# Router on the un-normalised sum, LayerNorm's scale and shift at evictions, a fourth likely expert

## What is computed

```python
h = layer_norm(ALPHA * h + mix, ln_g[i, 0], ln_b[i, 0])
ffn = hier_moe(h, group_w, group_b, expert_w, expert_b, gate_w, up_w, down_w)
h = layer_norm(ALPHA * h + ffn, ln_g[i, 1], ln_b[i, 1])

def hier_moe(t, ...):                      # 4 groups of 8 experts, D_FF = 512
    g_logits = t @ group_w + group_b       # the best group of each token
    g_prob = softmax(g_logits)             # its probability: g_val
    e_logits = t @ expert_w + expert_b     # within the group: the best two of 8
    top_p = softmax(top_v) * g_val
    hid = silu(t @ gate_w[e]) * (t @ up_w[e])
    out = sum over the token's two experts of top_p * (hid @ down_w[e])
```

## Time and profile before

| | |
|---|---|
| time, three runs | 1208.69, 1208.34, 1207.22 us |
| the profiled execution's own time | 1208.71 us |
| its span, first to last instruction | 1206.9 us |
| mean granted TensorE clock | 0.981 |
| TensorE busy | 1123.4 us (93%) |
| VectorE busy | 456.8 us (38%) |
| ScalarE busy | 318.2 us (26%) |
| GpSimd busy | 224.0 us (19%) |
| DMA moved | 427.14 MB |

### The profile page before, as it was taken

One profiled execution on the slowest core, in us unless ns is written; L12 is line 12 of the kernel. 1 busy time (PEld: TensorE's weight loads), 2 busy tenths in 40 slices (PEclk: granted clock), 3 DMA queues, 4 the chain that ended last, 5 costly groups with the idle time before them and its releaser, 6 DMA issues.

```text
span 1206.9 us, 16477 instructions
## 1 busy us (share of the span) xinstructions
PE 1123.4 (93%) x5664; PEld 665.5 (55%) x5664; DVE 456.8 (38%) x933; ACT 318.2 (26%) x590; POOL 224.0 (19%) x117
## 2 busy tenths in 40 slices
PE   8999999999999898899989899999999998899995
PEld 6998778643334444444343488875444454445552
DVE  3775773633322222222222344556332222222224
ACT  5578962221111011111111165632211111111110
POOL 2366775300000000000000388333000000000000
PEclk9999999999999999999999999998999999999998
DMA  9723559799999999999999933397999999999994
GB/s 367 288 105 113 201 193 367 277 370 398 432 428 427 430 428 428 428 429 428 428 428 424 413 116 140 140 370 320 390 410 430 428 428 428 429 428 428 428 425 188
DMA packets 35114, 427.14 MB, mean 354 GB/s; under 512 B 3728, under 2 KB 5936, under 8 KB 8064
## 3 DMA queue, kind: packets, MB, share of 16 engines
q1 hardware_dynamic: 32640, 416.13, 83.1%
q10 hardware_dynamic: 2240, 9.66, 2.2%
q0 software_dynamic: 192, 0.79, 0.4%
HBM read 424.69 MB, written 1.87 MB: 353 GB/s over the span
## 4 chain that ended last, share of the span: by engine, by line
PE 64%; DMA 22%; DVE 9%; ACT 2%; issue 2%; POOL 1%; ACTq 0%; SPq 0%; DVEq 0%; POOLq 0%
PE bank L844 26%; DMA ring<-in_gate_w 19%; PE bank L906 11%; PE bank L1009 4%; PE bank L592 3%; PE bank L728 3%; PE bank L1098 2%; DMA ring<-in_kv_w 2%; DMA reach_down<-in_down_w 1%; PE bank L1007 1%; PE bank L680 1%; PE bank L891 1%; PE bank L821 1%; DVE arena L1701 1%; PE bank L709 1%
## 5 line engine op out<-in xcount | busy, mean ns | idle before, releaser
L844 PE MATMUL bank<-ring,arena 128*64 128x512 f32 x928 | 417.2, 603 | 16.0 <-DMA ring<-in_gate_w 16.0
L906 PE MATMUL bank<-reach_down,arena 128*64 (+1 forms) x464 | 211.0, 607 | 29.1 <-DVE arena L1898 28.1
L541 POOL TENSOR_TENSOR split_ring<-ring,split_ring 128x1024 fp32r<-128x1024 f32 x56 | 138.5, 2503 | 461.9 <-ACT split_ring L534 456.7
L844 PE MATMUL bank<-reach_gate,arena 128*64 (+1 forms) x464 | 214.2, 610 | 0.0
L906 PE MATMUL bank<-ring,arena 128*64 128x512 f32 x464 | 210.7, 607 | 0.0
L844 PE MATMUL bank<-reach_up,arena 128*64 (+1 forms) x464 | 205.5, 595 | 0.0
L844 PEld LDWEIGHTS bank<-ring,arena 128*64 128x64 f32 x928 | 124.7, 138 | 134.9 <-issue 103.3
L1922 DVE TENSOR_TENSOR arena<-arena,bank 128x512 f32<-128x512 f32 x116 | 72.3, 682 | 194.8 <-PE bank L892 194.8
L906 PEld LDWEIGHTS bank<-reach_down,arena 128*64 128x64 f32 x464 | 61.9, 139 | 112.4 <-issue 102.5
L1915 DVE SCALAR_TENSOR_TENSOR split_arena<-bank,arena,split_arena 128x512 fp32r<-128x512 f32 x58 | 43.4, 750 | 150.0 <-ACT split_arena L1453 150.0
L844 PEld LDWEIGHTS bank<-reach_up,arena 128*64 128x64 f32 x464 | 60.9, 136 | 61.4 <-issue 60.5
(11 more groups left out here) (301 smaller groups left out, 1375.7 us busy)
## 6 DMA issues: line engine op xcount, KB each, us to landing
reach_gate<-in_gate_w SPq DMA_DIRECT2D x29, 2048.0 KB, 17.5
reach_up<-in_up_w SPq DMA_DIRECT2D x29, 2048.0 KB, 20.3
reach_down<-in_down_w SPq DMA_DIRECT2D x29, 2048.0 KB, 21.1
ring<-in_down_w SPq DMA_DIRECT2D x27, 2048.0 KB, 16.9
ring<-in_gate_w SPq DMA_DIRECT2D x25, 2048.0 KB, 17.9
ring<-in_up_w SPq DMA_DIRECT2D x25, 2048.0 KB, 16.8
ring<-in_in_w SPq DMA_DIRECT2D x9, 2048.0 KB, 21.5
ring<-in_out_w SPq DMA_DIRECT2D x4, 2048.0 KB, 9.1
```

Source lines behind the costliest of these rows:

```text
L541: unit.tensor_tensor(split_ring[:, j % RING, here], ring[:, j % RING, here], split_ring[:, (j + 1) % RING, here], ALU.subtract).then_inc(d ...
L844: last = mm(bank[out_bank][64 * e:64 * e + 64, :], exT[:, k, 64 * e:64 * e + 64], w, start=k == 0, stop=k == KD - 1)
L906: last = mm(bank[5 + c][64 * e:64 * e + 64, :], hidT[:, k, 64 * e:64 * e + 64], w, start=k == 0, stop=k == 3)
```

## The change

- The router multiplies the un-normalised sum ALPHA * h + mix. TensorE transposes it as soon as each quarter is added (`turn_mixed`, counted by `h_mixed`), all four copies out of PSUM are ScalarE's. `best_group` puts mean and deviation back with two instructions: the logits are (x @ w - mean * column sums of w) * rstd + folded bias. The column sums are a new reduction in `scale_router` and a new product in `fold_sum`.
- Gathered and sorted tokens are the normalised ones without scale and shift; these are applied where the tokens leave PSUM (`copy_exT`, now four instructions each on ScalarE and VectorE instead of one, and `store_sorted`). The old scalings at L1177, L1179, L1806 and L1812 go.
- ALPHA * (x * g + b) is made by VectorE in `residual` (two instructions for each 128 tokens); ScalarE's L1478 goes. The tokens' rest (L1194 on GpSimd) becomes `rest_of_tokens` on VectorE. Both are put in between other work of VectorE.
- The rows of scale and shift go to another home, and in layer 0 their load is issued after the last square of the SSD instead of with x.
- A fourth likely expert: `likely_fourth`, three rounds of five small instructions, for both layers. SyncE loads pair 1's second expert (the fourth likely one) and pair 2's first in interleaved halves (`first_halves`), and waits for the list by a signal given before `route`.
- `keep_clock` has five products instead of three before `rank`, and the ones between the last output blocks and the router go. GpSimd's preparation for the sort waits for `sel`.

```diff
...
@@ -412,6 +419,18 @@
     sp.dma_start(home, w[L, bass.ds(expert, 1), :, here].rearrange("e p x -> p (e x)")).then_inc(done, 16)
+
+def first_halves(L, base, before, kind, second, next_first):
+
+    j, ahead_j = slab_at(base, kind, 1), slab_at(base, kind, 0)
+    other = two_homes(sp, kind, 2)
+    for half in range(2):
+        here = slice(half * SLOT // 2, (half + 1) * SLOT // 2)
+        sp.wait_ge(w_used, before * 12 + (12 + 2 * (base - RING) + 4 * kind + 2 * half + 2))
+        fetch(L, second, kind, ring[:, j % RING, here], w_second[j % RING] if half else w_full[j % RING], here)
+        if half:
+            sp.wait_ge(w_full[ahead_j % RING], before * 16 + (32 + 16 * (ahead_j // RING)))
+        fetch(L, next_first(), kind, other[:, here], w_full[ahead_j % RING] if half else w_ahead, here)
@@ -442,7 +461,7 @@
 sp.wait_ge(moe[L]["first"], L + 1)
-return guesses(sp, L, 3)
+return guesses(sp, L, 4)
@@ -457,18 +476,27 @@
 sp.wait_ge(moe[L]["logit"], TB * (L + 1))
-sp.wait_ge(h_ready, 2 * L + 1)
 ahead(L, base, before, 1, 2, guess[2])
-sp.wait_ge(moe[L]["route"], L + 1)
-further = further_pairs(sp, L)
 def expert(i):
-def rest_of_pair(q, second, next_first=None, edge=None):
+def second_pair():
+    listed = []
+
+    def fifth():
+        if not listed:
+            sp.wait_ge(moe[L]["listed"], 2 * L + 2)
+            listed.append(expert(slice(4, 5)))
+        return listed[0]
+
+    for kind in range(2):
+        first_halves(L, base, before, kind, guess[3], fifth)
+    slab_of_pair(L, base, before, 1, 2, 1, guess[3])
+    ahead(L, base, before, 2, 2, fifth())
+
+def rest_of_pair(q, second, next_first=None):
     for kind in range(3):
-        slab_of_pair(L, base, before, q, kind, 1, second,
-                     halves=edge == ("last" if kind == 2 else "first"))
+        slab_of_pair(L, base, before, q, kind, 1, second)
         if next_first is not None:
@@ -478,8 +506,10 @@
+second_pair()
+sp.wait_ge(moe[L]["route"], L + 1)
+further = further_pairs(sp, L)
 turning = further * 2 // 3
-rest_of_pair(1, expert(slice(3, 4)), expert(slice(4, 5)), "first")
 with sp.Fori(1, turning - 1) as p:
@@ -645,7 +675,8 @@
 pe.wait_ge(fold_row, L + 1)
-mm(bank[3][:, 0:RC], ones, folded[:, L * RC:(L + 1) * RC], start=True, stop=True).then_inc(fold_mm, 1)
+mm(bank[3][:, 0:RC], ones, folded[:, L * RC:(L + 1) * RC], start=True, stop=True)
+mm(bank[3][:, 64:64 + RC], ones, less_sums[L], start=True, stop=True).then_inc(fold_mm, 1)
@@ -748,29 +779,34 @@
     for half in range(2):
-        if t == 0:
-            pe.wait_ge(hT_a, 7 * L + half + 1)
-        else:
-            pe.wait_ge(hT_v if half else hT_a, 3 * L + 1 if half else 7 * L + 3)
+        pe.wait_ge(hT_a, 8 * L + 2 * t + half + 1)
         for k in range(4 * half, 4 * half + 4):
-def turn_normed(L, t):
-
-    pe.wait_ge(xn_ready, 2 * L * TB + t + 1)
-    for k in range(KD):
-        b = bank[t_bank(2 * L) + 2 * t + k // 4]
+def turn_mixed(L, t, half):
+
+    pe.wait_ge(h_mixed, 2 * TB * L + 2 * t + half + 1)
+    for k in range(4 * half, 4 * half + 4):
+        b = bank[t_bank(2 * L) + 2 * t + half]
         last = nc.tensor.transpose(b[:, (k % 4) * P:(k % 4 + 1) * P], h[:, t, k * P:(k + 1) * P], ident)
-        if k % 4 == 3:
-            last.then_inc(hT_mm, 1)
+        if L == 0 and t == 0 and k == 0:
+            last.then_inc(w_used, 4)
+    last.then_inc(hT_mm, 1)
+
+def turn_and_route(L):
+
+    for t in range(TB):
+        for half in range(2):
+            turn_mixed(L, t, half)
+    for t in range(TB):
+        router_logits(L, t)
 last_blocks(1, 0)
-turn_normed(0, 0)
 def keep_clock(n, b):
@@ -781,9 +817,6 @@
 last_blocks(1, 1)
-keep_clock(1, 3).then_inc(w_used, 4)
-router_logits(0, 0)
-keep_clock(1, 3)
...
@@ -921,7 +957,7 @@
 m = moe[L]
-keep_clock(3, 6)
+keep_clock(5, 6)
 pe.wait_ge(m["mask"], L + 1)
@@ -935,7 +971,7 @@
 keep_clock(1, 6)
-pe.wait_ge(h_ready, L * 2 + 1)
+pe.wait_ge(xn_ready, 4 * L + TB)
 gather(L, 0)
...
@@ -1172,26 +1204,21 @@
-pool.wait_ge(ln_in, 32 * (n + 1))
+pool.wait_ge(ln_in, 32)
 pool.wait_ge(hT_mm, turned)
 last = T(h[:, t, :], h[:, t, :], lnw[:, 1, :], ALU.add)
-if n != 1:
-    last.then_inc(h_first, 1)
-elif t == TB - 1:
+if t == TB - 1:
     last.then_inc(h_ready, 1)
 m = moe[L]
-pool.wait_ge(mix_mm, 2 * TB * (L + 1))
+pool.wait_ge(m["sel"], L + 1)
 pool.memset(arena[:, lower_at + TB * D:lower_at + TB * D + CAP], 0.0)
   cst[:, C_BLK:C_BLK + 8].unsqueeze(2).to_broadcast([P, 8, CAP]), ALU.add).then_inc(m["low"], 1)
-pool.wait_ge(m["high"], L + 1)
-pool.wait_ge(m["route"], L + 1)
-T(h_low, h, h_high, ALU.subtract).then_inc(m["low"], 1)
@@ -1210,18 +1237,13 @@
     T(rs, rs, minus_half[:, 0:1], ALU.pow).then_inc(rstd_ready, 1)
-    if n == 0 and t == 0:
-        scale_shift(0, 0, 2, 1)
-if n == 2:
-    pool.wait_ge(xn_ready, TB * n + 2)
-    scale_shift(2, 0, 4 * n + 2, 4)
 if n in (0, 2):
     for t in range(TB):
-        scale_shift(n, t, 4 * (n + 1), 2 + t)
+        scale_shift(n, t, 4 * (n + 1), 1 + t)
     low_chunks(range(20, 24))
...
@@ -1383,6 +1402,8 @@
           accum_out=stats[:, g * TB + t:g * TB + t + 1]).then_inc(y_sq, 1)
+act.wait_ge(y_sq, G * TB)
+load_ln(0)
 for i in range(1, 4):
...
@@ -1466,16 +1494,13 @@
 A(rt[:, 72:74], rt[:, 72:74], ACT.Exp).then_inc(m["dexp"], 1)
-act.wait_ge(h_ready, L * 2 + 1)
+act.wait_ge(xn_ready, 4 * L + TB)
 A(h_high, h[:, :, :], ACT.Copy).then_inc(m["high"], 1)
-act.wait_ge(m["gathered"], 2 * L + 2)
-act.wait_ge(m["low"], 2 * L + 2)
-A(yacc[:, :, :], yacc[:, :, :], ACT.Copy, scale=ALPHA).then_inc(m["added"], 1)
 act.wait_ge(m["route"], L + 1)
...
@@ -1597,13 +1624,15 @@
 gain = cst[:, C_LNG + 2 * L * KD:C_LNG + (2 * L + 1) * KD]
-times(w, w, gain.unsqueeze(2).to_broadcast([P, KD, RC])).then_inc(fold_row, 1)
+link(times(w, w, gain.unsqueeze(2).to_broadcast([P, KD, RC])))
+V.tensor_reduce(less_sums[L], w.rearrange("p k c -> p c k"), AX.X, ALU.add).then_inc(fold_row, 1)
                 row[:, R_RB + L * RC:R_RB + (L + 1) * RC], ALU.add)
+V.tensor_scalar(less_sums[L], bank[3][:, 64:64 + RC], -1.0, None, ALU.mult)
@@ -1637,16 +1666,26 @@
+def likely_fourth(L):
+
+    at, same = prior_at, prior_same
+    for _ in range(3):
+        link(V.tensor_tensor(same[:, 2:5], at[:, 0:3], at[:, 3:4].to_broadcast([P, 3]), ALU.is_equal))
+        link(V.scalar_tensor_tensor(at[:, 3:4], same[:, 2:3], same[:, 3:4], at[:, 3:4], ALU.add, ALU.add))
+        link(V.tensor_tensor(at[:, 3:4], at[:, 3:4], same[:, 4:5], ALU.add))
+        link(V.tensor_scalar(same[:, 1:2], at[:, 3:4], E - 0.5, -1.0 * E, ALU.is_gt, ALU.mult))
+        link(V.tensor_tensor(at[:, 3:4], at[:, 3:4], same[:, 1:2], ALU.add))
 def likely_numbers(L):
     at, same = prior_at, prior_same
-    link(V.tensor_tensor(same[:, 4:7], at[:, 0:3], cst[:, C_K:C_K + 1].to_broadcast([P, 3]),
+    link(V.tensor_tensor(same[:, 4:8], at[:, 0:4], cst[:, C_K:C_K + 1].to_broadcast([P, 4]),
                          ALU.is_equal))
-    link(V.scalar_tensor_tensor(same[:, 2:3], same[:, 5:6], 2.0, same[:, 4:5], ALU.mult, ALU.add))
-    link(V.scalar_tensor_tensor(first_at[:, L:L + 1], same[:, 6:7], 3.0, same[:, 2:3], ALU.mult, ALU.add))
+    link(V.tensor_tensor(same[:, 4:8], same[:, 4:8], iota[:, 0:4], ALU.mult))
+    link(V.tensor_reduce(first_at[:, L:L + 1], same[:, 4:8], AX.X, ALU.add))
     link(V.scalar_tensor_tensor(threshold[:, L:L + 1], first_at[:, L:L + 1], 1.0e6,
                                 cst[:, C_THR:C_THR + 1], ALU.mult, ALU.add))
-    V.tensor_copy(first[:, L, 0:3], at[:, 0:3]).then_inc(moe[L]["first"], 1)
+    V.tensor_copy(first[:, L, 0:4], at[:, 0:4]).then_inc(moe[L]["first"], 1)
@@ -1682,6 +1721,8 @@
 if i == 15:
+    likely_fourth(0)
+if i == 16:
     likely_numbers(0)
...
@@ -1774,19 +1817,23 @@
 if n:
-    dve.wait_ge(h_ready, n)
+    dve.wait_ge(h_ready, 1)
 for t in range(TB):
     for c in range(2):
-        dve.wait_ge(mix_mm, (n // 2 * TB + t) * 2 + c + 1)
+        turn = (n // 2 * TB + t) * 2 + c + 1
+        dve.wait_ge(mix_mm, turn)
         cc = slice(c * 512, (c + 1) * 512)
-        link(V.scalar_tensor_tensor(h[:, t, cc], h[:, t, cc], ALPHA, mix(t, c), ALU.mult, ALU.add))
+        V.scalar_tensor_tensor(h[:, t, cc], h[:, t, cc], ALPHA, mix(t, c), ALU.mult,
+                               ALU.add).then_inc(h_mixed, 1)
+        dve.wait_ge(h_mixed, turn)
         column_sums(st, h, t, c)
     variance(st, t)
-    normalise(n, h, st, t)
+dve.wait_ge(rstd_ready, G + TB * n + TB)
+normalise(n, h, st, 0)
-dve.wait_ge(last_ln_in, 32)
+dve.wait_ge(last_ln_in, 96)
 for t in range(TB):
@@ -1794,22 +1841,31 @@
-def copy_turned(L):
+def first_choices(L):
     group_scores(0)
-    dve.wait_ge(hT_mm, 8 * L + 4)
-    V.tensor_copy(hT[:, 4:8, P:S], bank[t_bank(2 * L) + 3][:, :].rearrange("p (k s) -> p k s", k=4)
-                  ).then_inc(hT_v, 1)
     best_experts(0)
-    dve.wait_ge(ln_in, 32 * (2 * L + 1))
-    V.tensor_tensor(h[:, 1, :], h[:, 1, :], lnw[:, 0, :], ALU.mult).then_inc(h_scaled, 1)
-
-def shift_second(L):
-
```

(54 more changed lines are left out.)

96 lines of the change are left out of this document (57 added, 39 removed).

## The result

Six runs of the changed kernel gave 1211.99 us as the median (1210.56 to 1213.93), six of the kernel before 1208.51: a ratio of 1.0031, 95% interval 1.0018 to 1.0045. It is slower, by 2.2 to 5.4 us. It was measured twice more, on other chips, beside the experiments: 1.0059 (1.0042 to 1.0075) and 1.0045 (1.0026 to 1.0063). The mean of the three ratios is 1.0045, +5.4 us, where the first alone says +3.5 by its medians.

The account below looks back on a forecast made before the run. Transfers end each layer's experts, but with buffers full later TensorE's freeing of slots sets the stream. Layer 0's terms give +7.6 and layer 1's -3.2, together +4.4: 1213.1 profiled, 1212.7 us median, range 1204.5 to 1216.0.

Parts of the forecast that it names:

- Fourth expert, channel loop, +3.7: Ahead of tile 15's convolution in layer 0, 15 small VectorE instructions delay TensorE at tile 17: +3.7 us, bounds 1.7 and 4.2.
- the stand: In the channel loop, the new small VectorE instructions are kept out by GpSimd's instruction from 70.66 until 72.66.
- Rows of scale and shift, +2.45: Before the last output slab of layer 0, loading 1.05 MB of rows delays that slab: +2.45 us, bounds 0 and 3.2.
- Router, layer 0, -2.9: At layer 0's router, TensorE's counts end at 225.8 instead of 228.69: -2.9 us, bounds -2.0 and -3.9.
- layer 1, -3.65: At layer 1's router, TensorE's counts come at 825.2 instead of 828.85: -3.65 us, bounds -2.5 and -4.5.
- Filling, +0.45 per layer: Around each router, work put into VectorE's waits makes the list products late: +0.45 us, bounds 0 and 1.5; residual 0.
- Between pair 0 and 1, +3.9: In layer 0's experts, likely_fourth and column sums for layer 1 delay pair 1's hid: +3.9 us, bounds 3.4 and 4.5.
- the first rival: Transfers bound everywhere, so closed holes at the router count and the 3.9 does not: 1203.3 us, chance 0.17.
- SyncE, early list, 0: After the router, the first half can go at about 236.6 but then meets slots not yet free: 0.
- the fourth expert has its tokens: Rival denied here: a fourth expert without a token is still listed and may cost a pair, 29.4 us: 1242, chance 0.01.
- overflow: Rival: residual and the rest push pair 0's hid beyond TensorE's 1.65 us of sorting; 1216.7 us, chance 0.08.
- the mixer hides nothing: Rival denied here: no stand at 70.66 and the rows pass beside the slab, 1208.3 us, chance 0.20.

Follow-up runs that it names:

- spread0: Changed kernel with layer 0's 15 likely_fourth instructions five each ahead of tiles 15, 16 and 17, the numbers ahead of tile 18; 1217.94 us, 1.0073.
- without the fourth: Changed kernel with the 15 small instructions of likely_fourth left out in layer 0 alone; 1208.19 us, 1.0003 of the kernel before.
- early0: Changed kernel with 21 of layer 0's likely-expert instructions ahead of VectorE's first work, the other fourth rounds ahead of tiles 11 and 12; 1207.43 us, 0.9997.
- filled: Changed kernel with 22 unread products added on TensorE ahead of its wait for tile 17; 1211.78 us, 1.0025 of the kernel before.
- both of the best: The kernel best, and best with pair 1's second slabs issued only after the whole route is there; the latter 1202.05 us, 0.9942.
- experiment 3: Changed kernel with the first normalisation's scale and shift rows issued after the last eviction of the SSD output; 1212.99 us, 1.0043.
- best: Changed kernel with early likely experts in layer 0, layer 1's preparation inside pair 0, and scale and shift rows loaded later; 1202.28 us, 0.9959.
- prep_in_pair0: Changed kernel with layer 1's preparation moved into pair 0 of layer 0, nothing left out; 1212.60 us, 1.0033 of the kernel before.

## Why the prediction was right, and where its steps were not

Forecast 1212.7 and slower; measured 1211.99 and slower. The way and most of the terms are right; that the sum came so near is luck in part, as shown below. Step by step:

- **Fourth expert, channel loop, +3.7**: the delay is exactly that (table above), with the stand under GpSimd's second instruction. The rule of the Trainium skill on the shared ports (SBUF — State Buffer, "SBUF: two separate sides") that I weighed holds; four instructions of spread0 with two SBUF inputs show it again, by 0.68 to 1.96 us. **Missing was the second price.** In each of the seven traces with this pause, 3.51 to 3.55 us, tile 17's products take longer: 4.33 and 4.34 in two of them, 5.32 to 5.45 in five, against 3.09, so 1.25 or 2.3 us. In the traces without it (the kernel before, without the fourth, early, filled, both of the best) they take 3.09 to 3.13. Why it is one or the other is not shown. I had priced the pause by its length alone. The Trainium skill (TensorE: Matmul & The Clock Gate, "HAM oscillation — how this bites in real kernels") tells of a kernel whose TensorE waits so long between groups of products that each group starts at the lower clock. The trace agrees: the clock is 0.50 at 74 us, behind the pause. The term is 5.0 to 6.0.
- There is more of the same. From 140 to 160 us the clock is 0.78 to 0.84 in four of the eight traces with the pause (spread0 counted), and 1.00 in all six without. Over all runs the mean clock is 0.9798 to 0.9822 for the kernels with the pause, but for the first batch (0.9845), and 0.984 to 0.988 for those without. Whether the pause at 74 us brings on the dip at 150, and how, is not shown. The clock dips elsewhere without it: at the router (0.91 from 220 to 240 us) in four of the fourteen traces, two of which have no pause.
- **Rows of scale and shift, +2.45**: 1.7. Not all the bytes stand in front of the slab, and part of the cost is not bytes but ScalarE's two issues, which I had only in the upper bound. Shown by the traces of experiment 3 and of early0 beside best (1.4 on TensorE), not by a time.
- **Router, layer 0, -2.9; layer 1, -3.65**: -3.6 and -4.2 (from the shifts ahead of the routers, +6.85 and +7.4, to the counts' +3.2). All waits ahead of the counts are gone. But 828.85 in layer 1 stood behind six clock products of 5.47 us, where layer 0's six took 2.82, since the clock was 0.50 there. So 2.65 of the 4.2 us are a slow clock in the one execution before, and I had counted them as the change's. No experiment undid this part.
- **Filling, +0.45 per layer**: +0.3 in layer 0. `residual` ends at 251.84 and `hid` starts at 252.82, 0.97 us idle before it for TensorE, so nothing overflows, as counted.
- **Between pair 0 and 1, +3.9**: `hid` is 3.9 us later against pair 0's, and the slab 0.7 more: its transposes take 1.12 and its first products 1.11 us behind TensorE's pause of 4.17, with the clock at 0.50 from 289 to 295 us. Nearly all of it passes on: +8.1 at the slab is +7.5 at the attention, and of 3.75 us taken away 3.4 stay away. But of the 6.4 us that prep_in_pair0 and best take away only 4.1 and 3.8 are kept. So by these traces TensorE sets the stream for the first 4 us, and behind them the transfers do, as the first rival had it for the whole.
- **SyncE, early list, 0**: right, with the wrong reason. I had the first half going out at about 236.6; it went at 241.36, when TensorE freed the slot. In the changed kernel the hole at the router ends with TensorE's gate product, not with the list.

The forecast sum was near since the errors have both signs, and that is luck. In the profiled execution: +1.25 for the clock behind the pause, +0.7 for the clock at pair 1, +0.2 in the SSD, -0.75 for the rows, -1.25 for the routers, -0.7 for what the transfers swallow; 4.4 - 0.55 = 3.85, and the span is 3.8 later. The other two measurements, +5 and +8.5 us by their medians (+5.4 and +7.1 by the ratios), would be the same sum with larger dips of the clock; their mean clocks are lower (0.9822 and 0.9817, the first 0.9845), but that this is the cause is not shown. The stated range, 1204.5 to 1216.0, held a time without any loss as well, so what the result says for the mechanism rests on the traces. The rivals: the fourth expert has its tokens (no pair was added); overflow did not come; the mixer hides nothing.

## What to carry to other kernels

An instruction of four elements costs what it stands beside: 0.16 us alone, up to 2.3 us beside GpSimd, and more behind it if TensorE waits for it and loses its clock (1.25 or 2.3 us here). So small work that depends on little goes where its engine is idle and nobody waits: here 21 instructions ahead of VectorE's first work and 36 in a down product, with the later load of the rows, made a loss of 3.5 to 8.5 us into a gain of 5. Before one reads a difference of a few microseconds from one trace each, the clock must be compared by stretch: the dips differ from execution to execution by more than the change.
